# A two-block transformer on one Trainium2 core: the four feed-forward down-projections rewritten from plain tiled products to Strassen's scheme

## What is computed

```python
def swiglu(x, w_in, w_out):                      # layers 0 and 1, D_FF = 2816
    gate, up = jnp.split(x @ w_in, 2, axis=-1)
    return (jax.nn.silu(gate) * up) @ w_out

def conv_glu_ffn(h, w_up, conv_w, conv_b, w_down):   # layers 2 and 3, D_FF_2 = 2816
    u = causal_dwconv(jnp.einsum('btd,df->btf', h, w_up), conv_w, conv_b)
    gate, val = jnp.split(u, 2, axis=-1)
    return jnp.einsum('btf,fd->btd', jax.nn.silu(gate) * val, w_down)
```

## Time and profile before

| | us |
|---|---|
| median of 3 runs | 2623.61 (2623.51 to 2625.02) |
| span of the profiled execution, first to last instruction | 2621.6 |
| TensorE busy | 2589.7 (99%) |
| weight loads busy (beside TensorE) | 2317.5 |
| VectorE busy | 1360.3 (52%) |
| ScalarE busy | 1038.0 (40%) |
| GpSimd busy | 40.1 |
| moved by DMA | 235.76 MB, mean 90 GB/s |

### The profile page before, as it was taken

The page is one execution under the profiler, slowest core; times in us unless marked ns, Lnnn a source line. Parts: engine busy times, 40 slices in busy tenths (PEclk is TensorE's granted clock), DMA queues, the critical chain, the costliest instruction groups (busy, mean ns, idle before and its releaser), DMA issues.

```text
span 2621.6 us, 42668 instructions
## 1 busy us (share of the span) xinstructions
PE 2589.7 (99%) x18898; PEld 2317.5 (88%) x18898; DVE 1360.3 (52%) x2200; ACT 1038.0 (40%) x1702; POOL 40.1 (2%) x90
## 2 busy tenths in 40 slices
PE   9999999999999999999999999999999999999998
PEld 7777888888887888888899899999999989999998
DVE  6767533324656643333567456555245754655523
ACT  4554422213545432221455344444224534544421
POOL 0000000000100000000000000000000000000000
PEclk9999999999999999999999999999999999999999
DMA  5222222222312132222221132222232122222222
GB/s 190 89 61 71 95 97 95 87 96 77 111 64 80 65 108 90 93 92 101 83 104 66 58 106 81 97 83 92 89 110 105 66 68 96 97 82 96 93 89 77
DMA packets 40010, 235.76 MB, mean 90 GB/s; under 512 B 5536, under 2 KB 7840, under 8 KB 17936
## 3 DMA queue, kind: packets, MB, share of 16 engines
q1 hardware_dynamic: 35056, 214.45, 24.3%
q0 software_dynamic: 4048, 17.00, 1.9%
q10 hardware_dynamic: 720, 1.57, 0.2%
HBM read 222.38 MB, written 6.42 MB: 87 GB/s over the span
## 4 chain that ended last, share of the span: by engine, by line
PE 94%; DVE 4%; ACT 2%; DMA 0%; issue 0%; SPq 0%; DVEq 0%; ACTq 0%
PE P L557 77%; PE P L674 4%; PE P L652 3%; PE P L564 2%; PE P L686 1%; DVE WL L1850 1%; PE P L922 1%; PE P L943 1%; PE P L1036 1%; PE P L700 1%; PE P L732 1%; ACT WH L1285 1%; PE P L1088 0%; DVE X L1993 0%; DMA X<-in_xT 0%; PE P L1090 0%
## 5 line engine op out<-in xcount | busy, mean ns | idle before, releaser
L557 PE MATMUL P<-XH,WL 128*128 128x264 f32 (+3 forms) x3080 | 841.5, 322 | 12.4 <-DVE XL L2073 5.0
L557 PE MATMUL P<-XL,WH 128*128 128x264 f32 (+3 forms) x3080 | 822.5, 316 | 0.0
L557 PE MATMUL P<-XH,WH 128*128 128x264 f32 (+3 forms) x3080 | 820.0, 315 | 0.0
L1850 DVE TENSOR_TENSOR WL<-raw,WH 128x1024 fp32r<-128x1024 f32 (+2 forms) x405 | 483.0, 1195 | 536.3 <-ACT WH L1285 535.6
L1285 ACT ACTIVATE WH<-raw 128x1024 fp32r<-128x1024 f32 (+2 forms) x405 | 417.5, 1035 | 591.7 <-PE P L557 587.5
L557 PEld LDWEIGHTS P<-XH,WL 128*128 128x128 f32 x3080 | 519.8, 188 | 61.7 <-DVE XL L2073 6.9
L557 PEld LDWEIGHTS P<-XH,WH 128*128 128x128 f32 x3080 | 518.2, 188 | 38.0
L557 PEld LDWEIGHTS P<-XL,WH 128*128 128x128 f32 x3080 | 518.2, 188 | 36.4
L2549 DVE SCALAR_TENSOR_TENSOR tmp<-P,PP,tmp 128x527 f32<-128x527 f32 (+1 forms) x88 | 66.7, 758 | 195.3 <-ACT tmp L1795 195.3
L557 PE MATMUL P<-GHH,WL 128*128 128x264 f32 (+1 forms) x704 | 149.1, 283 | 0.0
L557 PE MATMUL P<-GHL,WH 128*128 128x264 f32 (+1 forms) x704 | 148.9, 282 | 0.0
(11 more groups left out here) (347 smaller groups left out, 3411.4 us busy)
## 6 DMA issues: line engine op xcount, KB each, us to landing
raw<-in_wts SPq DMA_DIRECT2D x167, 1024.0 KB, 4.9
raw<-in_wts SPq DMA_DIRECT2D x32, 896.0 KB, 4.6
spill<-X POOLq DMA_DIRECT2D x2, 2112.0 KB, 9.2
X<-spill POOLq DMA_DIRECT2D x16, 264.0 KB, 3.0
qswap<-qraw SPq DMA_DIRECT2D x44, 64.0 KB, 2.0
tab<-in_tR POOLq DMA_DIRECT2D x2, 1056.0 KB, 5.3
tmp<-in_biasT POOLq DMA_DIRECT2D x16, 128.0 KB, 2.9
tmp<-in_biasT POOLq DMA_DIRECT2D x16, 112.0 KB, 2.6
```

Of the source, the lines that this page charges most:

```text
L557: ins = nc.tensor.matmul(P[:, a:a + x1 - x0], wb[:, s, 128 * k:128 * k + 128], xb[:, kx, x0 - c0:x1 - c0], start=start and i == 0, stop=st ...
L1850: nc.vector.tensor_tensor(WL[:, u % NS, 0:length(u)], raw[:, u // 2 % RAW, a:a + length(u)], WH[:, u % NS, 0:length(u)].bitcast(F), ALU.su ...
```

## The change

Strassen's scheme (in Winograd's form) takes 2 x 2 blocks of a product and makes it with seven block products in place of eight. Here a block has two contraction tiles (a "pair" of 128 + 128 of the 2816 hidden features, 11 pairs), two output tiles (m = 2mp, 2mp+1) and the two halves of the tokens. Each of the seven products is a half-width matmul (256 tokens; 264 in g0) in three passes, accumulated over the pairs.

```diff
+UP_TILES = ((0, 12), (12, NF))
+PAIRS = ((0, 1, 2, 3, 4), (5, 6, 7, 8, 9, 10))
+SUMMED = {5: 0, 6: 1, 3: 2, 7: 3}
+ADDENDS = ((2, 0, 4), (3, 0, 3), (0, 1, 4), (1, 2, 3))
+AFTER = {6: 1, 7: 6, 4: 7, 3: 5}
+def order(ph, duo):
+    return (1, 2, 6, 7, 4, 5, 3) if (ph, duo) == (1, 1) else (1, 5, 2, 6, 7, 3, 4)
+def products(ph):
+    return [(p, 2 * duo + i) for duo in range(2) for p in order(ph, duo) for i in range(2)]
...
-        for m in range(NF):
-            cols(win, 128 * m)
-            cols(win, FF + 128 * m)
-        for m in range(8):
-            for k0, nk in ((0, 8), (8, 8), (16, 6)):
-                cols(wout, 128 * m, nk, k0)
+        for ph, (m0, m1) in enumerate(UP_TILES):
+            for m in range(m0, m1):
+                cols(win, 128 * m)
+                cols(win, FF + 128 * m)
+            for p, mp in products(ph):
+                plan.append(((wout, ph, mp, p), 0, len(PAIRS[ph]), 0, 128))
```

**Two phases.** Phase A stands after 24 of the 44 up tiles and covers pairs 0 to 4; phase B stands after the last 20 and covers pairs 5 to 10. Each phase has 28 units (7 products x 4 mp) of 5 or 6 stationary tiles (640 or 768 columns), each loaded by a DMA of its own:

```diff
+            def load_alone(u):
+                name, ph, mp, p = plan[u][0]
...
+                if p in SUMMED:
+                    sp.wait_ge(summed[mp], 16 * (len(ADDENDS) * (2 * st + ph) + 4))
+                    src = sums_dram[st, ph, mp, :, SUMMED[p], 0:n]
+                nc.sync.dma_start(raw_of(u), src).then_inc(unit_loaded[u % 4], 16)
...
+                if alone(2 * c):
+                    for u in (2 * c, 2 * c + 1):
+                        sp.wait_ge(*at("wlo", u - 2 * RAW))
+                        load_alone(u)
+                    continue
```

TensorE's new `down`. Products 1, 6, 7, 4 of one mp accumulate in one PSUM bank, 5 and 3 in another, and a later product waits for the eviction of the one before it in the bank:

```diff
+                for i, (p, mp) in enumerate(products(ph)):
+                    b, u = chain_bank(st, ph, p, mp), U + i
+                    if p in AFTER:
+                        pe.wait_ge(*at("ev", s, ph, mp, AFTER[p]))
+                    else:
+                        take(b)
+                    pe.wait_ge(*at("wlo", u))
+                    for q, j in enumerate(PAIRS[ph]):
+                        pe.wait_ge(*at("cl", s, j, PART[p]))
+                        for t, (wb, xb) in enumerate(((WL, CH), (WH, CL), (WH, CH))):
+                            ins = nc.tensor.matmul(P[:, 512 * b:512 * b + n], wb[:, u % NS, 128 * q:128 * q + 128],
+                                                   combined(st, xb, j, OPERAND[p]), ...)
```

**Weight sums.** Four of the seven weight operands are sums of the pair's four weight quadrants. GpSimd makes them by DMA from the new input `quads` into the new DRAM tensor `sums`, per stage, phase and mp, the first addend copied, three added:

```diff
+            def weight_sums(st):
+                for ph in range(2):
+                    n = 128 * len(PAIRS[ph])
+                    if ph:
+                        pool.wait_ge(*at("unit", first[STAGES[st] + "A"] + 27))
+                    for i, (q, a, b) in enumerate(ADDENDS):
+                        for mp in range(4):
+                            term = quads[st, ph, mp, :, q, 0:n].unsqueeze(1).broadcast_to([128, b - a, n])
+                            if i:
+                                pool.wait_ge(summed[mp], 16 * (len(ADDENDS) * (2 * st + ph) + i))
+                                nc.gpsimd.dma_start(sums_dram[st, ph, mp, :, a:b, 0:n], term, accum_op=ALU.add)...
+                            else:
+                                nc.gpsimd.dma_start(sums_dram[st, ph, mp, :, a:b, 0:n], term)...
+            pool.wait_ge(*at("res", 0, 7, 1))
+            weight_sums(0)
```

More of the change, by code:

```diff
@@ L389, in build @@
         raw_loaded = [semaphore(f"raw_loaded{i}") for i in range(RAW)]
+        unit_loaded = [semaphore(f"unit_loaded{i}") for i in range(2 * RAW)]
+        summed = [semaphore(f"summed{i}") for i in range(4)]
         x_loaded = [semaphore(f"x_loaded{k}") for k in range(8)]
@@ L598, in early_halves @@
                     between(1, k)
+                take(*late)
                 for ns in ((0, 1), (2,)):
@@ L781, in out_first, with norm_sums @@
                 work.finish()
-            def layer_norm(s, tiles, us, xh, xl, c0):
-                last = len(us)
-                for i in range(8 - last):
-                    b = whole_bank(s, i)
-                    if i >= 3:
-                        take(b)
-                    tiles(i, one(b))
-                    give((b,), ("res", s, tile_order(s)[i]))
+            def norm_sums(s, late, summed):
                 def mean(hf):
@@ new lines, in down_and_norm, with beside @@
+            def down_and_norm(st):
+                s = 2 * st + 1
+                mean, var = norm_sums(s, lambda hf: [(m, final(s, m, hf)) for m in ((4, 6) if hf else (5, 7))],
+                                      [("msum", s, "h", hf) for hf in range(2)])
+                def beside(kt):
+                    if kt == 3:
+                        mean(0)
+                    elif kt == 11:
+                        var(0, *range(8))
+                down(st, 1, beside)
+                return norm_rest(s, mean, var)
@@ new lines, in down_and_sums, with sums, beside, between @@
+            def down_and_sums(st):
+                s = 2 * st + 1
+                def sums(hf):
+                    take(6 + hf)
+                    pe.wait_ge(*at("ssum", s, "h", hf))
+                    ones_sum(ones_mean, rstd, sum_bank(s, hf), True, False)
+                    for m in (4, 6) if hf else (5, 7):
+                        pe.wait_ge(*at("xsq", s, m, hf))
+                        ins = ones_sum(ones_mean, tmp[m % 4], sum_bank(s, hf), False, m >= 6)
+                    ins.then_inc(*pe.up("ms", s, hf))
+                    give((6 + hf,), ("rln", s, hf))
+                def beside(kt):
+                    if kt == 7:
+                        sums(0)
+                down(st, 1, beside)
+                def between(phase, k):
+                    if phase == 0 and k == 3:
+                        sums(1)
+                return between if s < 7 else sums(1)
@@ L986, in residual @@
             def residual(s, tiles, us, xh, xl):
-                last = len(us)
-                for m in range(8 - last):
+                for m in range(6):
                     p = m % 3
@@ L2664, in pack_weights, with quadrant, pack_quads @@
             a += nk * n
+    return out
+def quadrant(w, pairs, mp, q):
+    c = 256 * mp + 128 * (q // 2)
+    return np.concatenate([w[256 * j + 128 * (q % 2):256 * j + 128 * (q % 2) + 128, c:c + 128] for j in pairs], 1)
+def pack_quads(w):
+    out = np.zeros((len(OUTS), 2, 4, 128, 4, 768), np.float32)
+    for st, name in enumerate(OUTS):
+        for ph in range(2):
+            for mp in range(4):
+                for q in range(4):
+                    out[st, ph, mp, :, q, 0:128 * len(PAIRS[ph])] = quadrant(w[name], PAIRS[ph], mp, q)
     return out
```

801 lines of the change are left out of this document (533 added, 268 removed), and 3 rows, old and new, of the table BANKS.

## The result

The changed kernel takes 2584.06 us (median of 4 runs, 2582.26 to 2587.22) against 2624.32 (4 runs, 2623.51 to 2625.04) for the kernel before on the same chip: ratio 0.9848, 95% interval 0.9834 to 0.9862. That is 40.3 us less, where the prediction had 44 and 2579.6.

What follows compares the result with a forecast made beforehand. TensorE was taken to bound the kernel (busy 2589.7 of 2621.6 us). Terms -59.0 + 9 + 2 + 4 = -44 us gave a span of 2577.6 and a median of 2579.6 us; own range 2564 to 2594, chance 0.67.

Steps and rivals of the forecast that it cites:

- matmuls: Four down-projections on TensorE: half-width products replace the old matmuls, 497.9 us becoming 438.9, a gain of 59.0 us.
- starts of phases: VectorE's leftover up-tile work delays each phase's fourth unit: 0.5 and 0 us in f stages, 2.4 and 1.6 in g; 9 us.
- phase A back to up tiles: After phase A the first 1 MB weight loads are right at the edge: 0.5 us for each of 4, 2 us.
- ends of stages: More evictions on VectorE at stage ends: 1.2 us at each of three junctions, 0.4 at the kernel's end; 4 us.
- weight sums: Accumulating DMAs in DRAM, hidden: phase B's take 99 us of 110 available in f0 and f1, 11 to spare.
- lower bound of 0.1160: Bound for a 256-wide matmul's step, half the 512-wide step; would give 6 us more gain than the 0.1181 taken.
- walk through VectorE: Instruction-by-instruction timing of VectorE from the last up tile's end to the fourth unit's conversion, giving the phase-start costs.
- f: In the weight sums, the cost of an added byte in copied ones; taken as 1.5.
- late began at 1.74: Phase B's weight sums come late from f = 1.74; the gain is gone at about f = 2.
- Half the rate for an addition: The skill's rule gives f = 2: phase B's sums 122 us, 12 late in f0 and f1, 7 in g0 and g1; 2618.
- rival (c): The ring of loads bounds phase A: landings of 6.2 us in place of 3.3, +29 us, 2608; chance 0.06.
- The signs named beforehand: Profile signs: phase step 0.118 (0.121 in g0), no idle TensorE, 2 us gaps at g's fourth units, near-zero SP waits for sums.

Runs made afterwards that it cites:

- e8_fewer: The changed kernel with the second of three passes left out for each unit's first pair (224 matmuls fewer): 2562.61 us, ratio 0.9764.
- e5_table: The changed kernel with ScalarE's function-table load for the norms moved from ahead of phase B's conversions to behind the ninth: 2579.63 us, ratio 0.9831.
- e2_spread: e5_table with the last pair's differences and splits also moved between each phase's first evictions: 2573.64 us, ratio 0.9804.
- e3b_sums_now: The changed kernel with phase B's weight sums started right behind phase A's, without waiting for phase A to end: 2618.89 us, ratio 0.998.
- e6_spread_junction: e2_spread with VectorE's conversion of WL for the next projection also made one tile earlier at a stage's end: 2571.82 us, ratio 0.98.
- e7_spread_g: e6_spread_junction with its edits in g0 and g1 alone, f0 and f1 as in the changed kernel: 2569.34 us, ratio 0.9791.
- e9_dense_g1: e7_spread_g with g1's combined activations 256 columns apart in memory, not 264: 2571.98 us, ratio 0.9797.
- e12_pause_f: e6_spread_junction with a TensorE wait for the third unit's eviction before the fourth unit of f0's and f1's phases: 2575.6 us, ratio 0.9813.

## Why the prediction came out right, step by step

| term | predicted, us | measured, us |
|---|---|---|
| matmuls (before: 497.9 predicted, 500.2 measured) | -59.0 | -68.6 |
| starts of phases | +9 | +14.0 |
| phase A back to up tiles | +2 | +2.1 |
| ends of stages | +4 | +5.2 (2.0 in the phases, 3.2 the rest outside them) |
| stretches at half clock | none | 4 x 1.5 = +6.0 |
| weight sums | 0 | 0 |
| sum | -44 | -41.3 (span: -41.1) |

The direction and the mechanism held: fewer matmuls on the engine that bounds the kernel, less what the seams cost. That the sum came within 4 us is in part luck. The matmuls gave 9.6 us more than reckoned, the seams took 27.3 us for 15 (starts, A to up tiles and ends as predicted in kind but 6.3 larger, and 6.0 of half clock that the prediction did not have), and the two errors nearly cancelled. The ends outside the phases are not measured one by one: they are what the balance leaves (8.3 us outside, less 2.1 and two stretches at 1.5), so the closing of the table tests only the part inside the phases, -49.6 by the terms for -49.4.

- **Matmuls.** The kernel before had 123.5 us of matmuls in each of f0 and f1, 128.0 in g0 and 125.1 in g1, start to start. 0.1215 and 0.1179 in g0 and g1 are near what the earlier trace rows gave (0.1208, 0.1181). In f0 and f1 the step was 0.1178 for the first 45 or 54 matmuls and 0.1134 for the rest, below the lower bound of 0.1160 (half of the 512-wide step): a half-width matmul there cost 0.486 of a full one (0.1134 of 0.2333). Two f stages of 924 are 210.4 us for the 218.2 reckoned. g0 at 112.3 and g1 at 108.9 complete 431.6. Weight loads, now one for each 0.1134 us at a listed 188 ns, did not hold the step at 0.118, as predicted; whether they set the 0.1134 is open, since e8_fewer takes a load away with each matmul.
- **Starts.** From the gaps less the steps they replace: 0.60 and 0.87 us in each f stage (0.5 and 0 predicted), 2.72 and 2.79 in phase A of g0 and g1 (2.4), 2.79 and 2.80 in B (1.6). (All but the last pair count the slow matmul right behind the gap in.) In A some 0.5 of it fell at the third unit, which the prediction had not named. Otherwise its walk through VectorE was right in A: the chain in g0 A goes convolution passes, multiply, `lows`, differences, then ScalarE's and VectorE's parts, as written. In B it left out the table load in ScalarE's queue, 0.9 us of the 1.2 it was short (e5_table).
- **Phase A back to up tiles.** The trace's chain at the end of f0 A is the one the prediction named: the first 1 MB load (issued at 443.66, 4.88 us), 1.07 us of ScalarE, 1.24 of VectorE, then the first up matmul at 450.94.
- **Half clock.** No row of before pointed to it, except at the kernel's very end. The prediction counted a gap at its own length; two of the four stretches hang on the starts of g0 B and g1 B, and went when those gaps shrank (e5_table) or closed (e2_spread).
- **Weight sums.** Phase B's took 97 us for the 99 reckoned, and nearly by the split reckoned. In the trace's packet records of queue q0, the copying in f0 lasted 26.1 us (452.2 to 478.3, 241 GB/s) for 26, the additions 73.5 (474.0 to 547.5, 150 GB/s) for 68 and 6 of rounds; the rounds themselves cost nothing, since four mp keep the engines at a share of 0.99. Over the four stages the additions moved 147 to 151 GB/s and the copies 224 to 256 beside the weights, so f by elapsed time is 1.5 to 1.7, where 1.5 was taken. It had been taken on an argument, with no row of an addition to settle it, and late began at 1.74. By the length of the packets an addition is dearer: one of 3072 bytes takes 253 ns, a copied one of 6144 bytes 234 (medians; means 255 and 274), 12.1 against 26.3 bytes a ns and engine. Why the two measures differ is not shown; what decides over lateness is the elapsed time.
- **Half the rate for an addition.** The Trainium skill ("Collectives: The Full Stack", why ReduceScatter is half of AllGather) has an add run at half the copy rate because of its two source reads. By packets the ratio here is 2.2 by medians and 1.9 by means, near that rule; by elapsed time it is 1.5 to 1.7, below it, and the end drawn from it (12 us late, 2618) did not come. The Trainium skill's 214 GB/s for copies between HBM tensors ("DMA: Bandwidth & Descriptors", the table of measured facts) was no ceiling here: in phase A, where the copying has the queues to itself (5.2 MB in 17.4 to 18.7 us), it moved 281 to 300 GB/s.
- **Loads.** Landings of 3.1 and 3.4 us for the 3.3 reckoned; rival (c) did not occur in the changed kernel, and did when the sums ran beside phase A (e3b_sums_now).
- **The signs named beforehand** came in the main as written: no idle TensorE in a phase after its start, gaps of 2.2 us (A) and 2.9 (B) at the fourth unit of g0's and g1's phases for the "about 2", last addition of f0's phase B at 547.8 us. The step of 0.118 came in g1, but in f0 and f1 only up to the fourth unit. SP did wait 10.7 us for sums, in 5 times with 4.4 the longest, and nothing behind it was late.

## What to carry to other kernels

When a scheme trades matmuls for work around them, price the seams and not the steady state: here the matmuls gave 69 us and the seams took back 27, of which 14.7 could be had again by moving a table load and the last tile's splits behind the first units of g0's and g1's phases, and one conversion forward at g0's end (2584.06 -> 2569.34 us). Follow *every* engine's queue across a seam, the one with the table load too. Bulk transfers inside DRAM were free here while large loads with slack ran beside them, and cost 35 us beside small loads on a ring that is only just deep enough, so when they run matters as much as how many bytes they move.

## What the runs showed of the hardware that was not expected

- A gap of TensorE of 2 to 3 us was followed in the changed kernel, four times, by 3.41 us at half the granted clock, which cost another 1.3 to 1.6 us where it could be compared. Not every gap of that length was: those of 2.2 us in g0 A and g1 A and one of 3.1 us at the end of f1 were not, nor the two of the kernel before there (1.95 and 3.09). Nor is that length needed: in e6_spread_junction, e7_spread_g, e9_dense_g1 and e12_pause_f the stretch behind g0 came with gaps of 1.2 us. What decides is not settled; the same code had the stretch at the end of f1 in some kernels and not in others.
- The same half-width matmul stream has two steady steps at full clock, 0.1178 and 0.1134 us (4%), which lasts to the end of a phase once taken. Only streams whose operands lay 256 tokens apart took the faster one, and only behind a short gap. It is worth 1.6 us a phase, so 6.6 us over the four, which is more than several of the effects studied here.
- An accumulating DMA in DRAM took 1.5 to 1.7 times a copy's time per byte by whole rounds and about twice by the length of its packets (253 ns for 3072 bytes, 234 for 6144), and TensorE's own work was not slowed beside DMA engines at a share of 0.99 (412 matmuls in 95 us, 411 at a share of 0.27).
